# A two-block transformer kernel on one core: the second half of two attention layers in a new order, by half slots

## The reference, cut to what matters

```python
def moba_attention(h, w_in, w_out):
    q, k, v = jnp.split(h @ w_in, 3, axis=-1)
    ...
    s_own = jnp.einsum('bhqd,bhkd->bhqk', q_c, k_own).astype(jnp.float32) * scale
    s_own = jnp.where(k_pos[None, :] <= q_pos[:, None], s_own, NEG_INF_2)
    p = jax.nn.softmax(s_own, axis=-1).astype(v.dtype)
    return jnp.einsum('bhqk,bhkd->bhqd', p, v_own)
def diff_attention(h, w_in, w_out, lam_q1, lam_k1, lam_q2, lam_k2, subln_g, lambda_init):
    ...
    p = jax.nn.softmax(s, axis=-1)
    w = (p[:, :, 0] - lam * p[:, :, 1]).astype(v.dtype)
    return jnp.einsum('bhqk,bhke->bhqe', w, v)
    ...
    o = rms_norm(o, subln_g) * (1.0 - lambda_init)
```

## Time and profile before

| what | value |
|---|---|
| median of 3 runs | 1231.46 us (1230.76 to 1231.69) |
| the profiled execution | 1230.47 us |
| its span, first to last instruction | 1228.7 us |
| PE busy, share of the span | 1200.2 us, 98% |
| DVE busy | 948.5 us, 77% |
| ACT busy | 618.5 us, 50% |
| mean granted TensorE clock | 0.996 |

### The profile page before, as it was taken

The page is one execution under the profiler, slowest core; times in us unless marked ns, Lnnn a source line. Parts: engine busy times, 40 slices in busy tenths (PEclk is TensorE's granted clock), DMA queues, the critical chain, the costliest instruction groups (busy, mean ns, idle before and its releaser), DMA issues. The chain is left out here.

```text
span 1228.7 us, 14780 instructions
## 1 busy us (share of the span) xinstructions
PE 1200.2 (98%) x5795; PEld 984.6 (80%) x5795; DVE 948.5 (77%) x1371; ACT 618.5 (50%) x841; POOL 100.4 (8%) x138
## 2 busy tenths in 40 slices
PE   7999999999999999999999999999999997999997
PEld 6888887888778878888887768888888776888885
DVE  6789878876656689888786668898998787766656
ACT  7445336445764464343565556344346664634441
POOL 2010132001600010000000000000100000000000
PEclk9999999999999999999999999999999999999999
DMA  9999995644655489989466437788855642567540
GB/s 308 339 317 320 315 301 180 222 141 160 198 169 174 160 295 338 311 302 322 137 233 207 135 115 259 265 288 301 316 193 200 190 138 103 170 204 226 176 166 35
DMA packets 145206, 274.31 MB, mean 223 GB/s; under 512 B 6241, under 2 KB 76081, under 8 KB 145137
## 3 DMA queue, kind: packets, MB, share of 16 engines
q1 hardware_dynamic: 127280, 209.80, 50.7%
q0 software_dynamic: 17792, 63.56, 15.3%
q10 hardware_dynamic: 64, 0.02, 0.0%
HBM read 270.41 MB, written 2.93 MB: 222 GB/s over the span
## 5 line engine op out<-in xcount | busy, mean ns | idle before, releaser
L1472 DVE TENSOR_TENSOR lo_w<-w_raw,hi_w 128x2048 fp32r<-128x2048 f32 x197 | 448.0, 2287 | 70.5 <-ACT hi_w L1035 70.2
L1035 ACT ACTIVATE hi_w<-w_raw 128x2048 fp32r<-128x2048 f32 x197 | 374.2, 1916 | 42.9 <-DMA w_raw<-in_w_mix_out 11.6
L498 PE MATMUL ps<-hi_w,xT 128*128 128x512 f32 x912 | 365.8, 401 | 5.8 <-DVE xT L1494 3.4
L500 PE MATMUL ps<-lo_w,xT 128*128 128x512 f32 x912 | 357.1, 392 | 0.0
L499 PE MATMUL ps<-hi_w,xT 128*128 128x512 f32 x912 | 356.5, 391 | 0.0
L498 PEld LDWEIGHTS ps<-hi_w,xT 128*128 128x128 f32 x912 | 172.2, 189 | 46.1 <-issue 11.1
L500 PEld LDWEIGHTS ps<-lo_w,xT 128*128 128x128 f32 x912 | 171.8, 188 | 37.2
L499 PEld LDWEIGHTS ps<-hi_w,xT 128*128 128x128 f32 x912 | 172.4, 189 | 33.4
L498 PE MATMUL ps<-hi_w,hT_hi 128*128 128x512 f32 x480 | 188.5, 393 | 0.4 <-DVE hT_lo L1682 0.4
L500 PE MATMUL ps<-lo_w,hT_hi 128*128 128x512 f32 x480 | 187.0, 390 | 0.0
L499 PE MATMUL ps<-hi_w,hT_lo 128*128 128x512 f32 x480 | 186.9, 389 | 0.0
(11 more groups left out here) (265 smaller groups left out, 1041.9 us busy)
## 6 DMA issues: line engine op xcount, KB each, us to landing
w_raw<-in_ffn_w_in SPq DMA_DIRECT2D x86, 512.0 KB
aux<-in_ada_w POOLq DMA_DIRECT2D x34, 1024.0 KB, 6.9
w_raw<-in_mlp_w_up SPq DMA_DIRECT2D x32, 1024.0 KB
w_raw<-in_mlp_w_down SPq DMA_DIRECT2D x32, 1024.0 KB
w_raw<-in_w_mix_in SPq DMA_DIRECT2D x26, 1024.0 KB
w_raw<-in_ffn_w_out SPq DMA_DIRECT2D x22, 1024.0 KB
area<-in_ada_w POOLq DMA_DIRECT2D x14, 1024.0 KB, 5.7
w_raw<-in_moba_w_in SPq DMA_DIRECT2D x12, 1024.0 KB
```

The source lines that it names most:

```text
L498: pe.matmul(dst, lhs_hi, rhs_hi, start=start, stop=False)
L500: return pe.matmul(dst, lhs_hi, rhs_lo, start=False, stop=stop)
L1035: act.activation(hi_w[:, ring_slot(u), :], w_raw[:, ring_slot(u), :], ACT.Copy).then_inc(w_hi, 1)
L1472: vec.tensor_tensor(lo_w[:, ring_slot(u), :], w_raw[:, ring_slot(u), :], hi_w[:, ring_slot(u), :].bitcast(F32), ALU.subtract).then_inc(w_l ...
```

## The change

- The table now ends at slot 9. The events of slots 10 to 13 are new for both layers: scores and weights stand half a slot to a whole slot earlier, W(7) and O(7) have moved out of slot 14 into slot 13, and in DIFF so has T(2). `busy` is gone. In DIFF T(3) stands behind both quarters (0,0,0) and (1,0,0), before it stood between them.
- The copy of the last transposed keys goes from DVE (`heads_out(3)`, L2054) to ACT (`last_heads_out`).
- DIFF: the norm of chunks 0 to 3 computes its root factor once over 8 columns (`first_rstd`), before twice over 4 (`norms`); the two multiplications remain (`first_norm`).
- ACT and DVE have a written-out order from slot 10 on. In it units 14 and 15 are split early, units 16 to 18 late. In DIFF `split_lo(u0 + 18)` is cut in two halves, one before and one after `pair_los(3)` (`split_lo_half`).
- W(7) in MoBA and W(4) in DIFF no longer wait until the outputs before them are out (nor does W(0), whose wait had nothing to wait for). In DIFF slot 12 now waits for four split chunks, before for two. `low_ready(u)` is a new name for the wait on `w_lo`.

Line numbers in the new file differ by a few from those of the profile.

```diff
@@ -124,11 +124,11 @@
 ATTENTION = [(0, [], []), (1, [], []), (2, [], []), (3, [], ["H0"]), (4, [], ["H1"]), (5, [], ["S0"]),
              (6, [], ["S1", "W0"]), (7, [], ["S2", "O0", "W1"]), (8, [], ["S3", "O1", "W2"]),
-             (9, ["H2"], ["O2", "W3"]), (10, ["H3"], ["S4", "O3"]), (11, ["S5", "T0"], ["T1", "W4"]),
-             (12, ["S6"], ["O4", "W5"])]
-MOBA_SLOTS = ATTENTION[:11] + [(11, ["S5"], ["W4"]), (12, ["S6"], ["O4", "W5"]), (13, ["S7", "O5", "W6"], ["O6"]),
-                              (14, [], [])]
-DIFF_SLOTS = ATTENTION + [(13, ["S7"], ["O5", "W6", "O6"]), (14, [], [])]
+             (9, ["H2"], ["O2", "W3"])]
+MOBA_SLOTS = ATTENTION + [(10, ["H3", "O3"], ["S4"]), (11, ["S5"], ["W4", "S6"]), (12, ["O4", "W5", "S7"], ["O5", "W6"]),
+                          (13, ["O6", "W7"], ["O7"]), (14, [], [])]
+DIFF_SLOTS = ATTENTION + [(10, ["H3", "O3"], ["S4"]), (11, ["S5", "T0", "T1"], ["W4", "S6"]),
+                          (12, ["O4", "W5", "S7"], ["O5", "W6"]), (13, ["O6", "W7"], ["O7", "T2"]), (14, [], [])]
 PAIR_BANK, NORMED = (4, 5, 0, 1), (1, 2, 3, 4)
 N_PIECE = 24
 PIECES = (8, 9, 7)
@@ -902,7 +905,7 @@
                     pe.wait_ge(at_p, ab + c)
-                    if c % 4 == 0 or c == 7 and not diff:
+                    if c == 4 and not diff:
@@ -952,12 +955,6 @@
-                def busy(b, n):
-
-                    pe.wait_ge(at_m, ab + 8)
-                    for _ in range(n):
-                        pe.matmul(ps[:, b * BANK:b * BANK + SEQ], xT_hi[:, 0, 0:P], xT_hi[:, 0, :], start=True, stop=True)
-
@@ -980,7 +977,7 @@
                                 if slot == 12 and t == 0 and diff:
-                                    pe.wait_ge(ch_lo, ch_o + 2)
+                                    pe.wait_ge(ch_lo, ch_o + 4)
@@ -989,19 +986,12 @@
                                     do[event[0]](int(event[1:]))
                     elif slot == 14:
-                        weights_T(7)
-                        if not diff:
-                            busy(1, 4)
-                        outputs(7)
-                        if diff:
-                            busy(0, 6)
-                            outputs_T(2)
-                        pe.wait_ge(w_lo, u0 + 15)
+                        low_ready(u0 + 14)
                         last_quarter(0, 0, 0)
+                        low_ready(u0 + 15)
+                        last_quarter(1, 0, 0)
                         if diff:
                             outputs_T(3)
-                        pe.wait_ge(w_lo, u0 + 16)
-                        last_quarter(1, 0, 0)
                         last_quarter(0, 0, 2).then_inc(part_done, 1)
                         last_quarter(1, 0, 2).then_inc(part_done, 1)
                         for n in range(2):
@@ -1381,64 +1371,79 @@
...
+                def last_heads_out():
+                    act.wait_ge(headT, hb + 4)
+                    act.wait_ge(headT_out, hb + 3)
+                    act.activation(k2T[1], bank(0, 2).rearrange("p (c n) -> p c n", c=4), ACT.Copy).then_inc(headT_out, 1)
+
...
+                project_out(4)
+                weights_out(3)
+                taken(2)
+                split_hi(u0 + 14)
+                last_heads_out()
+                taken(3)
+
+                exps(4)
                 if diff:
+                    pair_his(0)
+                    pair_his(1)
+                    exps(5)
+                    split_hi(u0 + 15)
+                else:
+                    split_hi(u0 + 15)
+                    exps(5)
+
+                weights_out(4)
+                project_out(5)
+                exps(6)
+                if diff:
+                    squares(4)
+                    weights_out(5)
+                    split_hi(u0 + 16)
+                    exps(7)
+                    squares(5)
+                    weights_out(6)
+                    split_hi(u0 + 17)
                     act.activation(table_in[:, 3:4], table_in[:, 0:1], ACT.Sqrt)
+                    norm_root_of(0)
                     squares(6)
                     weights_out(7)
-                    norm_root_of(0)
                     squares(7)
+                    pair_his(2)
                     norm_root_of(1)
-                    pair_his(2)
+                    split_hi(u0 + 18)
                     pair_his(3)
+                else:
+                    weights_out(5)
+                    output_hi(4)
+                    exps(7)
+                    weights_out(6)
+                    output_hi(5)
+                    split_hi(u0 + 16)
+                    weights_out(7)
+                    output_hi(6)
+                    split_hi(u0 + 17)
+                    output_hi(7)
                     split_hi(u0 + 18)
-                else:
-                    output_hi(6)
-                    split_hi(u0 + 18)
-                    weights_out(7)
-                    output_hi(7)
@@ -1471,6 +1476,18 @@
+
+            def split_lo_half(u, h):
+
+                cols = slice(h * UNIT // 2, (h + 1) * UNIT // 2)
+                vec.wait_ge(w_hi, u + 1)
+                ins = vec.tensor_tensor(lo_w[:, ring_slot(u), cols], w_raw[:, ring_slot(u), cols],
+                                        hi_w[:, ring_slot(u), cols].bitcast(F32), ALU.subtract)
+                if h == 0:
+                    steps.inc(ins)
+                else:
+                    steps.wait(vec)
+                    ins.then_inc(w_lo, 1)
@@ -2099,17 +2116,18 @@
-                def norms(c, n):
-
-                    k = c % 4
-                    vec.wait_ge(at_out, c + n)
-                    vec.wait_ge(at_norm, c // 2)
-                    squares = head_sq[:, k:k + n, :]
-                    then(vec.tensor_tensor(squares, squares, head_eps[:, k:k + n, :], ALU.add))
-                    rsqrt(head_rstd[:, 0:NT * n], squares.rearrange("p c t -> p (c t)"), NT * n, 1.0 / P, 0.0)
-                    heads = o2[:, :, c * P:(c + n) * P].rearrange("p t (c n) -> p t c n", c=n)
-                    factor = head_rstd[:, 0:NT * n].rearrange("p (c t) -> p t c", t=NT).unsqueeze(3)
-                    vec.tensor_tensor(heads, heads, factor.broadcast_to([P, NT, n, P]), ALU.mult).then_inc(at_norm, 1)
+                def first_rstd():
+
+                    vec.wait_ge(at_out, 4)
+                    then(vec.tensor_tensor(head_sq[:, :, :], head_sq[:, :, :], head_eps[:, :, :], ALU.add))
+                    rsqrt(head_rstd[:, :], head_sq[:, :, :].rearrange("p c t -> p (c t)"), 4 * NT, 1.0 / P, 0.0)
+
+                def first_norm(n):
+
+                    vec.wait_ge(at_norm, n)
+                    heads = o2[:, :, 2 * n * P:(2 * n + 2) * P].rearrange("p t (c n) -> p t c n", c=2)
+                    factor = head_rstd[:, 2 * NT * n:2 * NT * (n + 1)].rearrange("p (c t) -> p t c", t=NT).unsqueeze(3)
+                    vec.tensor_tensor(heads, heads, factor.broadcast_to([P, NT, 2, P]), ALU.mult).then_inc(at_norm, 1)
@@ -2156,77 +2174,87 @@
...
+                outputs(2)
+                rotate(3)
+                split_lo(u0 + 14)
+                outputs(3)
                 if diff:
+                    first_rstd()
+                    first_norm(0)
+                    scores(4)
+                    first_norm(1)
+                    scores(5)
+                    combine(4)
+                    pair_los(0)
+                    pair_los(1)
+                    scores(6)
+                    combine(5)
+                    split_lo(u0 + 15)
+                    outputs(4)
+                    combine(6)
+                    scores(7)
+                    split_lo(u0 + 16)
+                    combine(7)
                     outputs(5)
-                    combine(7)
+                    last_sums(0)
+                    split_lo(u0 + 17)
                     outputs(6)
-                    last_sums(0)
                     last_rstd(0)
                     last_norm(0)
                     outputs(7)
                     last_sums(1)
+                    pair_los(2)
                     last_rstd(1)
-                    pair_los(2)
                     last_norm(1)
+                    split_lo_half(u0 + 18, 0)
                     pair_los(3)
+                    split_lo_half(u0 + 18, 1)
+                else:
+                    scores(4)
+                    shares(4)
+                    scores(5)
+                    split_lo(u0 + 15)
+                    scores(6)
+                    shares(5)
+                    outputs(4)
+                    shares(6)
+                    scores(7)
+                    shares(7)
+                    outputs(5)
+                    split_lo(u0 + 16)
+                    outputs(6)
+                    split_lo(u0 + 17)
+                    outputs(7)
                     split_lo(u0 + 18)
-                else:
-                    shares(7)
-                    outputs(6)
-                    split_lo(u0 + 18)
-                    outputs(7)
```

(91 more changed lines are left out.)

22 lines of the change are left out of this document (10 added, 12 removed).

## The result

The changed kernel takes 1223.37 us (median of 4 runs, 1223.17 to 1223.46) against 1231.11 us (4 runs, 1230.18 to 1231.69) of the kernel before measured beside it: 7.7 us less, ratio 0.9936 with a 95% interval of 0.9924 to 0.9948. The forecast was 1223.3, 8.2 us less.

A forecast was written before the change was run, and what follows sets the result against it. PE, busy 98% of the span, was taken as the bound, losing time in both attention tails, norms and clock. MoBA 2.3 + DIFF 4.5 + clock 1.4 = 8.2 us less, 1223.3 us; range 1221.6 to 1227.2, about 85%.

The forecast's parts named there:

- The tail of MoBA: O(6) to slot 14 in MoBA: all 2.4 us of waits and filler go, net 2.3 us less.
- Late next in MoBA: Norm behind MoBA: DVE's split of unit 18 ends 0.1 to 0.2 us after the norm's input is there.
- DIFF up to slot 14: DIFF before slot 14: 3.55 us from removed tail waits and filler plus 0.45 from small waits, together 4.0 us.
- the small waits of slots 10 and 11: PE's waits before T(1) and W(4) in DIFF, freed by DVE's savings: 0.45 us, between 0 and 0.9.
- The walk: Following the three engine queues through slots 10 to 14 with known durations: no new wait, tightest at outputs(5) before O(6).
- T(3) behind both quarters: DIFF tail: T(3) directly before matmuls needing its chunks leaves its copies uncovered, cost 1.4 us.
- The cut split: DIFF norm: unit 18's split just fits around the norm's input, so the gain at L575 is 4.5 us.
- The clock: DIFF norm: PE no longer idles before L575, granted clock stays 1.00, 1.4 us more gained; bounds 0 to 1.4.
- Rival A: Clock falls anyway, with filler gone and uncovered waits in the DIFF tail: 1224.7 to 1226.1 us, chance 16%.
- B: Rival: a handoff misses by a weight split, PE waits up to 2.2 us once per layer: 1225.5 to 1227.7, 15%.
- C: Rival: slower, outputs(4) on DVE holds up later chunks, which run one at a time: 1238 us, 5%.
- D: Rival: the change does nothing much, the DIFF norm being held by something else: 1231 us, 3%.

The follow-up runs named there:

- e6: Changed kernel with S(6) before W(4) and S(7) before W(5) in both layers: 1223.26 us.
- e10: Changed kernel with the copy of the last keys back on DVE in both layers: 1223.78 us.
- e11: Changed kernel with the last keys' copy back on DVE and, in DIFF, the norm of chunks 0 to 3 in two parts again: 1225.09 us.
- e5: Changed kernel with T(3) of DIFF between the first and second quarter, as before: 1221.94 us.
- e3: Kernel before, with only DIFF's split of unit 18 altered: ACT's copy ahead of the last pair's copies, DVE's subtraction cut in two: 1228.25 us.
- e4: Changed kernel with the split of unit 18 in DIFF whole and behind the last pair again, on both engines: 1225.92 us.
- e1: Changed kernel with the old order in DIFF, so only MoBA has the new one: 1230.15 us over 11 runs.
- e8: Changed kernel with six unread matmuls behind T(2) and six behind T(3) in DIFF: 1222.77 us.
- e7: Changed kernel with DVE's split of unit 16 in DIFF one place earlier, before the maxima of chunk 7: 1225.64 us.

## Why the prediction was right, and where it was off

*The total.* 8.2 us were forecast, 7.7 to 7.8 measured. The signs and places of all steps hold; three sizes are off. That the time itself came within 0.1 us (1223.3 for 1223.37) is partly luck: beside the changed kernel the old one took 1231.11 us, 0.35 less than the median that the forecast started from. And two of the misses go against each other: MoBA gave 0.6 us less than forecast, DIFF up to its norm 0.2 more.

*The tail of MoBA,* forecast 2.3: measured 1.8 at the norm's transposes and 1.7 at the end of the layer. The waits went as forecast. The step that was mis-sized is "All 2.4 us go": I took the small events at their prices in the earlier trace rows, where each stands beside a half slot. In the new order three stand in front of another small event and cost more: H(3) 1.02 us before O(3), for 0.84 before; W(4) 0.75 before S(6), for 0.58; W(5) 0.81 before S(7), for 0.63. That is 0.5 us, all of the gap. e6 shows that the neighbour is the cause (0.63 for both W), and that the price can't simply be avoided.

*Late next in MoBA,* DVE's split of unit 18: forecast to end 0.1 to 0.2 us too late. The norm starts directly behind it, at 726.90, where 722.35 + 4.43 = 726.78 was possible: 0.1 us.

*DIFF up to slot 14,* forecast 4.0 us. Counted from the second tile's transposes behind MoBA (743.78 before, 742.82 after), the first matmul of slot 14 comes 4.35 us earlier. T(2) waits 0.28 us for the norm (forecast 0.25), and T(2) to the quarter takes 1.93 (2.0). The term for the small waits of slots 10 and 11, put at 0.45, was the one too small, by 0.3 us: from H(3) to O(4) the new order is 0.76 us shorter (20.56 us before, 16.94 after, which has one half slot of 2.86 less in it), and from O(4) on 3.6 (forecast 3.55).

*DVE's two savings* in that term: e10 and e11 put them at 0.8 us for the keys' copy alone and 2.1 for both. So the second is worth 1.3 us once the copy is on DVE. What the new order would have cost without them is more than what the waits of before were worth; they were a condition of the new order rather than a gain of their own. The walk was wrong for one (0 to 0.3 instead of 0.8), because it looked at T(1) and not at S(5) in front of it, and right for both together (1.9 for 2.1) in the sum only: it had put all of it at T(1), and in the trace 0.7 us are lost at S(5) and 1.4 at T(1). The second saving alone, with the keys on ACT, was not tried.

*T(3) behind both quarters,* forecast +1.4: e5 gives back 1.2, and 0.2 more is T(3)'s wait for the norm where it stands between.

*The cut split,* norm 4.5 us earlier: 4.7 at L575 against L578, of which e3 and e4 assign 1.8 and 1.7 us to the split's place (copy and subtraction together).

*The clock,* 1.4: exactly that from L575 to the second tile (10.71 before, 9.33 after), and shown from both sides by e3 and e4. The size is no independent hit: it is the drop of the same trace from which the term was worked out, and with the drop of e1 it would be 2.8. Rival A is refuted for this kernel: the granted clock was 1.00 through both uncovered waits, and filler there (e8) changes nothing. The drop comes with the idle time in front of L575: of the 13 traces the three that have it (before, e1, e4) show a clock below 1 in the DIFF norm, and the ten without it take 9.29 to 9.34 us from these transposes to the second tile. The Trainium skill (TensorE: Matmul & The Clock Gate, "What's actually happening") says that the throttled clock is the default and that activity releases it; e3, e4 and the norm of before agree with it, e8 shows that it gives no reason to fill every gap.

*No new handoff wait* (against B): right, with margins of 0.33 us before O(6) in DIFF (forecast 0.3) and 0.76 in MoBA (`outputs(5)` ends at 716.41, O(6) starts at 717.17; forecast 0.4). e7 shows what B costs when it comes true: 2.5 us in one layer, over the 2.2 that I gave it, since T(2) waits 0.3 us longer too. C and D did not occur.

## What to carry to other kernels

Where one engine is the bound, read its starts and not its busy share, and walk the queues of the others through the new order: what counts is which item of work that nobody is waiting for (here a weight split) stands in front of one that is waited for. Starting such an item's copy earlier, cutting the rest in two and moving half of it into a wait was worth 3.2 us here, more than the whole new order of the MoBA layer. Before a chunk of work is moved next to another small one, price the pair, not the single pieces.

## What the runs showed of the hardware that I had not expected

The length of the clock drop differed between two executions with the same order of work in the layer: 3.4 us at 1.2 GHz in the trace of before, 6.8 in e1, whose DIFF layer is that of before; the loss was 1.4 and 2.8 us. The idle times in front of it were the same: 1.57 and 1.07 us in e1, 1.59 and 1.07 before. What sets the length is open.

Two idle times of 1.30 and 1.21 us, 2.9 us of work apart, left the clock at 1.00 (changed kernel), while 1.55 and 1.07 us with only eight transposes between them brought it down (e4).

Six transposes followed by small matmuls on 64 rows take 0.12 to 0.18 us longer than the same six followed by a matmul of 512 columns (0.75 and 0.81 us, 0.63). The three transposes of a DIFF chunk show it too: 0.42 and 0.25 us.
